# Two layers of a hybrid encoder on one core: the output projection's tiles in the order 0,4,1,5,2,6,3,7, and the query rotation's temporary in another buffer

## The reference

```
for each layer:
  h = rms_norm(x, g_mix);  z = h @ w_in          # split: q_lat | c_kv | k_r | u | v
  q = (rms_norm(q_lat, g_q_lora) @ w_q_up)       # 8 heads of 64 + 32
  q = concat(rms_norm(q[:64], g_qn), apply_rope(rms_norm(q[64:], g_qr)))
  k, v from rms_norm(c_kv) @ w_kv_up (and a cache of 1024 positions for the sample)
  o_att = block_causal_attention(q, k, v);  o_gm = spatial_gating(u, v)
  x = x + concat(rms_norm(o_att), rms_norm(o_gm)) @ w_o        # 1024 -> 1024
  h2 = rms_norm(x, g_ffn)
  x = x + (silu(h2 @ w_gate) * (h2 @ w_up)) @ w_down           # 1024 -> 2816 -> 1024
```

## Time and profile before

| | us |
|---|---|
| median of 3 runs (1446.21 to 1470.13) | 1446.27 |
| the profiled execution | 1442.24 |
| its span | 1440.4 |
| PE busy | 1347.2 (94%) |
| DVE busy | 942.7 (65%) |
| POOL busy | 865.2 (60%) |
| ACT busy | 585.2 (41%) |
| chain that ended last: PE, DVE, ACT, POOL | 76%, 14%, 3%, 2% |

### The profile page before, as it was taken

One profiled execution on the slowest core, in us unless ns is written; L12 is line 12 of the kernel. 1 busy time (PEld: TensorE's weight loads), 2 busy tenths in 40 slices (PEclk: granted clock), 3 DMA queues, 4 the chain that ended last, 5 costly groups with the idle time before them and its releaser, 6 DMA issues.

```text
span 1440.4 us, 25402 instructions
## 1 busy us (share of the span) xinstructions
PE 1347.2 (94%) x9448; PEld 1238.5 (86%) x9448; DVE 942.7 (65%) x1526; ACT 585.2 (41%) x953; POOL 865.2 (60%) x460
## 2 busy tenths in 40 slices
PE   6998979987999999999999989789699999999998
PEld 6885656887999999999998756669699999999997
DVE  3456577388677666666736585764967777777775
ACT  4235457334333333333342354663443333333331
POOL 3645147365777777777655443364567777777771
PEclk9999999998999999999999999999899999999999
DMA  7110010030223333222421000111223222222221
GB/s 225 59 37 11 5 59 30 31 88 30 89 89 92 96 96 93 89 87 87 129 87 51 26 5 10 51 60 31 58 86 91 88 87 87 87 87 87 87 87 66
DMA packets 130257, 102.35 MB, mean 71 GB/s; under 512 B 8844, under 2 KB 116816, under 8 KB 130192
## 3 DMA queue, kind: packets, MB, share of 16 engines
q1 hardware_dynamic: 127528, 100.46, 22.8%
q10 hardware_dynamic: 2664, 1.02, 0.3%
HBM read 98.10 MB, written 3.36 MB: 70 GB/s over the span
## 4 chain that ended last, share of the span: by engine, by line
PE 76%; DVE 14%; ACT 3%; POOL 2%; issue 2%; DMA 1%; SPq 0%; ACTq 0%; DVEq 0%; POOLq 0%
PE ps L2201 33%; PE ps L1909 7%; PE ps L1913 7%; PE ps L1910 7%; PE ps L1892 3%; PE ps L1893 3%; PE ps L1894 3%; PE ps L1854 3%; PE ps L2142 3%; PE ps L2122 2%; POOL rs L746 2%; DVE hs_lo L1299 1%; PE ps L2006 1%; DVE tm L1451 1%; PE ps L2099 1%
## 5 line engine op out<-in xcount | busy, mean ns | idle before, releaser
L746 POOL TENSOR_TENSOR rs<-ms,mhalf 128x8 f32<-128x8 f32 (+5 forms) x66 | 140.5, 2132 | 218.9 <-DVE ms L1429 82.4
L845 POOL TENSOR_TENSOR w_lo<-raw,w_hi 128x1024 fp32r<-128x1024 f32 x132 | 228.4, 1757 | 50.7 <-ACT w_hi L1250 39.6
L1682 DVE TENSOR_REDUCE raw<-raw 128x512 f32<-128x1024 f32 x184 | 231.2, 1258 | 1.7 <-DMA raw<-in_w_gate 1.4
L845 POOL TENSOR_TENSOR w_lo_a<-raw,w_hi_a 128x512 fp32r<-128x512 f32 x88 | 178.5, 2040 | 75.3 <-ACT w_hi_a L1250 70.2
L1909 PE MATMUL ps<-act_hi,w_hi 128*128 128x288 f32 x704 | 195.8, 293 | 3.5 <-issue 3.5
L1910 PE MATMUL ps<-act_lo,w_hi 128*128 128x288 f32 x704 | 196.0, 294 | 0.0
L2201 PE MATMUL ps<-t_hi,w_hi 128*128 128x288 f32 x528 | 159.0, 301 | 25.3 <-DVE t_lo L1669 20.7
L1644 DVE TENSOR_TENSOR xT<-ps,xT 128x576 f32<-128x576 f32 x192 | 143.0, 755 | 58.8 <-PE ps L1913 58.7
L2201 PE MATMUL ps<-t_lo,w_hi 128*128 128x288 f32 x528 | 157.8, 299 | 0.0
L2201 PE MATMUL ps<-t_hi,w_lo 128*128 128x288 f32 x528 | 157.6, 298 | 0.0
L1913 PE MATMUL ps<-act_hi,w_lo 128*128 128x288 f32 x704 | 150.4, 295 | 0.0
(11 more groups left out here) (243 smaller groups left out, 3483.8 us busy)
## 6 DMA issues: line engine op xcount, KB each, us to landing
raw<-in_w_gate SPq DMA_DIRECT2D x88, 256.0 KB, 3.8
raw<-in_w_up SPq DMA_DIRECT2D x88, 256.0 KB, 3.8
raw<-in_w_down SPq DMA_DIRECT2D x20, 1024.0 KB, 4.8
raw<-in_w_in SPq DMA_DIRECT2D x10, 1024.0 KB, 5.3
raw<-in_w_o SPq DMA_DIRECT2D x8, 1024.0 KB, 5.1
x_tm<-in_x_prompt SPq DMA_DIRECT2D x4, 512.0 KB, 5.0
raw<-in_w_down SPq DMA_DIRECT2D x8, 256.0 KB, 3.4
out_y_prompt<-x_tm SPq DMA_DIRECT2D x8, 256.0 KB, 2.2
```

Source lines behind the costliest of these rows:

```text
L746: pool.tensor_tensor(rs[:, c:c + n], ms[:, c:c + n], mhalf[:, 0:n], ALU.pow).then_inc(rs_ready, 1)
L845: pool.tensor_tensor(lo[:, k, cols], src, hi[:, k, cols].bitcast(F32), ALU.subtract).then_inc(lo_split, 1)
L1682: dve.tensor_reduce(raw[:, 2, j * Q:(j + 1) * Q], added(a, b), AX.X, ALU.add).then_inc(sums_added, 1)
```

## The change

The tiles of the output projection are made in the order 0,4,1,5,2,6,3,7 on all engines (`W_O_ORDER`), so each load of w_o brings two pieces of 128 columns in two DMAs (512 KB each, where one had 1024 KB). On VectorE each pair of adds is followed by its `x_sum` and `x_low`; the sums of w_gate come later, between `add(2)` and `add(6)`. ScalarE's and GpSimd's lists are put in a matching order; GpSimd waits for all four `t_lo` before the last sum of squares. The rotation's first temporary moves from `sq` to columns of `raw` behind the query weight (1536 to 1791 of its slot), ScalarE's wait for `tile_normed` goes, and the first load of w_o, which takes that slot, waits for the last query's rotation.

The diff, cut:

```diff
+W_O_ORDER = [j + e * KT // 2 for j in range(KT // 2) for e in range(2)]
...
-        L["w_o"] = [slots.load() for _ in range(4)]
+        L["w_o"] = [slots.load(dmas=2) for _ in range(4)]
...
                 for j, n in enumerate(L["w_o"]):
-                    load(n, by_k(n, COLS), a["w_o"][l][:, j * COLS:(j + 1) * COLS].rearrange("(k p) n -> p k n", p=P))
+                    if j == 0:
+                        sp.wait_ge(tile_normed, PREPS * l + max(t["seq"] for t in L["preps"] if t["what"] == "q") + 1)
+                    load(n, *((by_k(n, COLS)[:, :, f * P:(f + 1) * P],
+                               a["w_o"][l][:, m * P:(m + 1) * P].rearrange("(k p) n -> p k n", p=P))
+                              for f, m in enumerate(W_O_ORDER[2 * j:2 * j + 2])))
...
                 low_piece(gate_in, 1)
-                sum_squares(2 * l + 1, [4])
+                sum_squares(2 * l + 1, [4, 5])
                 for no in range(2, PIECES):
                     low_piece(gate_in, no)
-                sum_squares(2 * l + 1, [5])
                 low_piece(up_in, 0)
                 low_piece(up_in, 1)
-                sum_squares(2 * l + 1, [6, 7])
+                sum_squares(2 * l + 1, [6])
+                pool.wait_ge(t_lo_done, KT // 2 * (l + 1))
+                sum_squares(2 * l + 1, [7])
                 low_piece(up_in, 2)
...
                         if seq == 0:
                             act.wait_ge(rq_ready, l + 1)
-                        elif L["preps"][seq - 2]["what"] == "q":
-                            act.wait_ge(tile_normed, PREPS * l + seq - 1)
...
                 square_output(0)
+                x_scale(0)
                 square_output(1)
                 w_high(L["w_o"][2])
+                t_high(0)
                 square_output(2)
+                x_scale(1)
                 square_output(3)
-                x_scale(0)
-                x_scale(1)
                 w_high(L["w_o"][3])
+                t_high(1)
                 for no in range(2):
                     high_in(gate_in, no, None, 0)
                 square_output(4)
-                t_high(0)
+                x_scale(2)
+                square_output(5)
                 for no in range(2, PIECES):
                     high_in(gate_in, no, slots.last[L["w_o"][2]], SUMS * l)
-                square_output(5)
-                t_high(1)
-                x_scale(2)
+                t_high(2)
                 for no in range(2):
                     high_in(up_in, no, None, 0)
                 square_output(6)
                 x_scale(3)
-                t_high(2)
-                filled(act, L["wo"][-1][1])
+                filled(act, L["wo"][W_O_ORDER[-1]][1])
...
-                        parts = (sq[:, seq % 2, :, NOPE:QK], rot[:, :, :])
+                        turned = raw[:, L["wq"] % 2, 2 * HEADS * QK:2 * HEADS * QK + HEADS * ROPE]
+                        parts = (turned.rearrange("p (h c) -> p h c", h=HEADS), rot[:, :, :])
...
-                for m in range(4):
-                    add(m)
+                for k in range(2):
+                    add(k)
+                    add(k + KT // 2)
+                    x_sum(k)
+                    x_low(k)
+                add(2)
                 for j in range(4):
                     sum_in(j, gate_in, None, 0)
-                add(4)
-                x_sum(0)
-                x_low(0)
-                add(5)
-                x_sum(1)
-                sum_in(0, up_in, gate_in, 1)
-                x_low(1)
-                sum_in(1, up_in, gate_in, 1)
                 add(6)
                 x_sum(2)
                 x_low(2)
+                add(3)
+                for j in range(2):
+                    sum_in(j, up_in, gate_in, 1)
                 add(7)
                 x_sum(3)
```

More of the change, by code:

```diff
@@ L323, in build_plan @@
         L["mt"] = {k: ring.add("merged_out") for k in MERGED}
-        L["w_o"] = [slots.load() for _ in range(4)]
+        L["w_o"] = [slots.load(dmas=2) for _ in range(4)]
         if len(ring.units) % 2:
             ring.skip()
-        L["wo"] = [[ring.add("wo_added", with_last=h > 0) for h in range(2)] for _ in range(KT)]
+        L["wo"] = {m: [ring.add("wo_added", with_last=h > 0) for h in range(2)] for m in W_O_ORDER}
         for j, n in enumerate(L["w_o"]):
-            slots.used(n, L["wo"][2 * j + 1][1])
+            slots.used(n, L["wo"][W_O_ORDER[2 * j + 1]][1])
         def down_units(n, y=None):
@@ L628, in _, with load @@
         def _(sp):
-            def load(n, dst, src):
+            def load(n, *parts):
                 if n >= 2:
@@ L635, in load @@
                         sp.wait_ge(lo_split, slots.ready[n - 2])
-                sp.dma_start(dst, src).then_inc(raw_loaded[n % 2], 16)
+                for dst, src in parts:
+                    sp.dma_start(dst, src).then_inc(raw_loaded[n % 2], 16)
             def by_k(n, cols, count=KT):
@@ L665, in _ @@
                         sp.wait_ge(sums_added, SUMS * l)
-                    load(n, by_k(n, c1 - c0, (rows.stop - rows.start) // P), in_cols(l, rows, c0, c1))
+                    load(n, (by_k(n, c1 - c0, (rows.stop - rows.start) // P), in_cols(l, rows, c0, c1)))
                     if l == 0 and n == L["w_in"][1]:
@@ L922, in high_part, with square @@
                                ).then_inc(hs_hi_done, 1)
-            def square(m, k):
-                if k >= 2:
-                    act.wait_ge(summed, m * KT + k - 1)
-                act.activation(gate[:, k % 2, :], xT[:, k, :], ACT.Square).then_inc(squared, 1)
+            def square(m, no, k):
+                if no >= 2:
+                    act.wait_ge(summed, m * KT + no - 1)
+                act.activation(gate[:, no % 2, :], xT[:, k, :], ACT.Square).then_inc(squared, 1)
             for l, L in enumerate(plan):
@@ L940, in _ @@
                     if l:
-                        square(2 * l, k)
+                        square(2 * l, k, k)
                 w_high(L["w_in"][1], KT * KV_KR)
@@ L944, in _ @@
                     for k in range(KT):
-                        square(0, k)
+                        square(0, k, k)
                 def prep_first(t):
@@ L1145, in t_high, with square_output @@
                     act.activation(t_hi[:, :, k, :], x_sums[:, k % 2, :, :], ACT.Copy).then_inc(t_hi_done, 1)
-                def square_output(k):
+                def square_output(no):
+                    k = W_O_ORDER[no]
                     emptied(act, L["wo"][k][0])
-                    square(2 * l + 1, k)
+                    square(2 * l + 1, no, k)
                 def x_scale(k):
@@ L2145, in _, with out_tile @@
                         ins.then_inc(full, 1)
-                def out_tile(m, ks=None):
-                    by_feature(L["wo"][m], slots.raw[L["w_o"][m // 2]] % 2, m % 2 * P, COLS, KT, hs_hi, hs_lo,
-                               order=MERGED[1:], ks=ks, ready=None if m else lambda k: emptied(pe, L["mt"][k]))
+                def out_tile(no, ks=None):
+                    by_feature(L["wo"][W_O_ORDER[no]], slots.raw[L["w_o"][no // 2]] % 2, no % 2 * P, COLS, KT, hs_hi, hs_lo,
+                               order=MERGED[1:], ks=ks, ready=None if no else lambda k: emptied(pe, L["mt"][k]))
                 pe.wait_ge(gm_normed, NT * (l + 1))
@@ L2160, in _ @@
                         split_ready(L["w_o"][0])
-                        for w in L["wo"][0]:
+                        for w in L["wo"][W_O_ORDER[0]]:
                             free(w)
@@ L2184, in _ @@
                 out_tile(0, MERGED[5:])
-                for m in range(1, KT):
-                    split_ready(L["w_o"][m // 2])
-                    for u in L["wo"][m]:
+                for no in range(1, KT):
+                    split_ready(L["w_o"][no // 2])
+                    for u in L["wo"][W_O_ORDER[no]]:
                         free(u)
-                    out_tile(m)
+                    out_tile(no)
                 def product(u, weights, k_w, x, first, ks=range(KT // 2), ready=None):
```

6 lines of the change are left out of this document (3 added, 3 removed).

## The result

The changed kernel took 1434.95 us in the median (1422.94 to 1449.95), before took 1449.28 us beside it (1441.96 to 1470.13): a ratio of 0.987, 95% interval 0.983 to 0.991. It is 1.3% faster, within the 2% band. The range forecast (1421 to 1437) holds the median; the forecast itself, 1429, is 6 us too low. Executions of one kernel lie up to some 30 us apart, by how long TensorE's granted clock stands at 0.50; in the traces the difference lies in the prompt attention, which the change does not touch.

The account below looks back on a forecast made before the run. TensorE, busy nearly the whole span, was taken as the bound, so only its waits could shrink, the longest 20.7 us for `t_lo`. 2 x (2.5 + 6.1) = 17.2 us off gave a 1429 median, range 1421 to 1437.

Parts of the forecast that it names:

- Part B: Rotation's temporary moved to `raw`, so ScalarE squares query tiles without waiting: 2.5 us per layer, bounds 1.0 and 3.7.
- steps 1 to 3: Adds, `x_sum`s and `t_lo`s of the output projection in the new order: last `t_lo` at 327.6, 9.2 us earlier.
- One sentence on the way there: VectorE operations with both inputs in SBUF wait for the whole GpSimd operation that they meet.
- Step 4: Behind the last `t_lo`, GpSimd's sum of squares and w_up piece delay the low parts: 0.5 plus 2.1 = 2.6 us.
- Step 5: TensorE starts the FFN block at 317.1, works 3.6 us, rests some 4 for `hs_lo`; a clock fall shows about 0.5.
- the two terms of 0.5 us: Given back behind the last `t_lo`: 0.5 us for GpSimd's last sum of squares, 0.5 for TensorE's clock falling.
- part A: New tile order of the output projection: 9.2 - 2.6 - 0.5 = 6.1 us per layer gained.
- one shift, 4 us: Profiled execution of before lay 4 us under its median; the same shift turned 1425 profiled into 1429 median.
- the release of all contention: Rival: VectorE's operations fall between GpSimd's, TensorE loses nearly all its waits in the block; 30 us, 1416; chance 0.08.
- The lock: Rival: the two later `x_sum`s take 7.7 us each beside GpSimd's stream; total gain 1.6 us, 1445; chance 0.10.
- TensorE never waited inside the projection: Slower rival: w_o's fourth piece comes late and TensorE stops inside the projection; 14 us slower, 1460; chance 0.03.

Follow-up runs that it names:

- split and tail: Changed kernel, GpSimd's third and fourth w_o subtractions cut into four, its w_up piece moved behind the root and `r_tok` copy: ratio 0.981 to before, median 1423.9.
- the split: Changed kernel, GpSimd's third and fourth w_o subtractions cut into four of 512 columns: 79.18 us from first add to first `act_lo`, 2.4 less, single execution.
- the tail's run: Changed kernel, GpSimd's w_up piece moved behind the root and the copy of `r_tok`: 1.2 us faster in all at equal lost clock.
- the two runs of one and the same program: Changed kernel with the rotation's lines as before, so only the tile order is changed, measured twice: ratios 0.985 and 0.991 to before.
- changed with ACT's wait kept: Changed kernel, rotation's temporary in the new buffer but ScalarE still waiting for the tile's norm: ratio 0.992 to before.
- the rotation alone: Kernel before with only the rotation's temporary moved and ScalarE's wait changed, tiles in the old order: ratio 0.998 (0.994 to 1.003).

## Why the prediction was right or wrong

**Part B: right.** Forecast 2.5 us per layer, measured 2.0 to 2.45 in layer 0 and 2.45 in layer 1 (4.1 to 5.6 in all at no loss, by the pair of kernels). ScalarE's two waits for `tm` are gone; instead it waits 0.69 and 0.78 us for TensorE:

```profile
183.59 0.58 ACT L969 ACTIVATE sq<-ps,r_q 128x384 f32<-128x384 f32 x1 [0.69 <-PE ps L2012]
...
190.31 0.58 ACT L969 ACTIVATE sq<-ps,r_q 128x384 f32<-128x384 f32 x1 [0.78 <-PE ps L2012]
```

**Part A, steps 1 to 3: right.** Counted from the first add, the four `t_lo`s were forecast at 17.1, 29.8, 44.7 and 54.7 us and came at 17.1, 30.0, 45.3 and 55.0. The last one is 8.9 us earlier than before, against 9.2. Each w_o subtraction met one operation of `x_sums` (4.89 and 4.95 us); with both cut in four the last `t_lo` came 2.5 us earlier. One sentence on the way there says more than its rows: it speaks of VectorE operations with both inputs in SBUF, and the copy of the earlier trace rows, which was held 4.55 us, has one input.

**Step 4: the mechanism right, the price too high.** The low parts behind the last `t_lo` took 4.39 us instead of 2.27, 2.1 more against 2.6. The w_up piece's own hold was priced right: the same low parts take 2.1 us less in split and tail (second row), where the piece comes later, than in the split (first row).

```profile
324.52 4.99 DVE L1307 SCALAR_TENSOR_TENSOR hs_lo<-xT,gT,hs_hi 128x576 fp32r<-128x576 f32 x3
...
324.23 2.88 DVE L1308 SCALAR_TENSOR_TENSOR hs_lo<-xT,gT,hs_hi 128x576 fp32r<-128x576 f32 x3
```

But only half of it is on the path: without it A falls by 0.7 to 1.2 us. The forecast charged all of it to TensorE's idle time, though TensorE has work of its own there (the 0.90 us that VectorE waits for it in the tail's run).

**Step 5: happened.** TensorE rests 4.2 us for `hs_lo` (4 forecast), and the clock is at 0.50 in the slice behind it:

```profile
322.00:324.00 2.00, 0.47 (x3) 0.51 (x4) 2.00 (x5) 1.37 (x2) 0.00 (x0) 0.93 0.00 0
324.00:326.00 2.00, 2.00 (x10) 2.00 (x10) 2.00 (x4) 1.48 (x3) 0.00 (x0) 0.50 0.03 8
326.00:328.00 2.00, 2.00 (x13) 1.88 (x11) 1.28 (x3) 1.08 (x2) 1.99 (x2) 0.72 0.00 0
```

All that is given back behind the last `t_lo` is 1.8 us per layer (26.7 us from it to `act_lo`, before 24.9), where steps 4 and 5 had 3.1. So part A is 7.1 us and not 6.1. Of the 1.8 about one is the w_up piece's. The slow clock behind the `hs_lo` wait adds nothing that shows: the split has no such stretch (its clock is 1.00 from 211 to 340 us), and its distance from the last `t_lo` to `act_lo` is 26.65 us all the same. As I read the traces, the two terms of 0.5 us, for the sum of squares and for the clock, lie in one place and were counted twice. In the changed kernel and in the tail's run VectorE waits 0.72 us for TensorE's first `side`; in split and tail it does not, but the low parts take 2.88 us, 0.6 more than before, beside the sum of squares, and 0.5 us are given back.

**The sum: 17.2 forecast, 18.9 to 19.0 measured** where both kernels run undisturbed (2 x 7.15 by the distances and 2 x 2.3 for part B, 19.0 by the fastest executions).

**The median: 6 us too low, and this is the step that failed.** I took one shift, 4 us, from the profiled execution of before to its median and used it for the changed kernel too. The gap between a kernel's fastest execution and its median is 7.4 us for before but 12.3 for the changed kernel. So of the 19 us 14.1 arrive in the median (1449.2 to 1435.1). The other 4.9 us fit the stretches in the prompt attention: one at 0.50 costs 6.6 us in the profiled execution (the first layer is 9.1 us ahead, the second only 2.5), and 18 of 23 executions of the changed kernel were long ones, of before 37 of 68. Of the 6 us some 3 come from the starting point alone, since the median of three executions of before (1446.3) stood 2.9 us under that of all 68 (1449.2); the other 3 are the 14.1 that arrived in place of 17.2. Nothing in the range allowed for the clock, so that the median still fell inside it, 2 us from its upper end, is in part luck.

Whether the change makes them more frequent is not settled. All kernels in which ACT's wait is gone together had 45 long executions of 60, all in which it stands 56 of 110. That is more than chance alone would give if executions were independent, but the two runs of one and the same program gave 1 of 6 and 7 of 12, the closest pair (changed, and changed with ACT's wait kept) 18 of 23 and 7 of 12, and my expectations built on it missed for three kernels. The traces show how thin the edge is (two waits of 0.95 us that end near 227 and 230 us in both traces, with and without a fall), not what tips it. If the link is real, part B's 4.6 us are mostly paid for: the rotation alone was no faster in the median.

The rivals: the release of all contention did not come (even split and tail leave 2.4 us of `hs_lo`). The lock did not eat the gain: `x_sum(2)` and `x_sum(3)` took 5.3 and 2.9 us (4.9 and 2.7 forecast), since they met shorter pieces. TensorE never waited inside the projection.

## What to carry to other kernels

Where one engine's operations wait for another engine's running instruction, as VectorE's do for GpSimd's here, look at the longest instruction that a critical operation can meet, and not at the other engine's total: cutting it gave 2.4 us per layer, though the total grew, while holding the other engine back moved most of the collision to a later operation. Count distances inside the trace, from an event ahead of the changed code to one behind it; for one order of work they repeated within 0.2 us where totals vary by 30. And forecast a median from the spread of many executions, not from one profiled execution, when TensorE's clock has stretches at half speed nearby.

## What the runs showed of the hardware

The wait of VectorE's two-input operations is for the instruction that GpSimd is running, and ends with it: 4.89 us beside one of 4.61, 1.56 beside one of four that together take 6.39. The Trainium skill, page "SBUF — State Buffer", section "Who interferes with whom", says so (an exclusive lock for the whole instruction), and adds that a reduction never contends: by that sentence the trace agrees. In the changed kernel one `TENSOR_REDUCE` takes 1.24 to 1.28 us where GpSimd rests (40 of them) and 1.24 to 1.27 where it is busy throughout (94). It makes the price of a collision a matter of the other engine's tile size.

The second surprise is the clock. During the second of two waits of 0.95 us TensorE's granted clock went from 2.4 to 1.2 GHz, at 229.2 us, and stayed there until 256.5 us, although every slice from 232 to 256 us shows it busy for 4.00 of 4.00 us. In another execution of the same program the same waits had no such effect. The Trainium skill, page "TensorE: Matmul & The Clock Gate", section "What's actually happening", says that the gate's look at the activity is not tied to the kernel's start, which could make such falls differ between executions; no run here shows the gate itself.
